# Casting DMAs that wait for transposing DMAs in a two-layer decoder trunk on eight cores

## What is computed

```
for l in (0, 1):
    x = LN(alpha*x + 0.5 * swiglu(x, w_gate_up[l,0], w_down[l,0]))     # hidden width 2816
    y = hgrn2(x) if l == 0 else fox(x, k, v, c)
    x = LN(alpha*x + y)
    x = LN(alpha*x + 0.5 * swiglu(x, w_gate_up[l,1], w_down[l,1]))
    if l == 0: k, v, c = shared_kv(x)
```

## Time and profile before

| | |
|---|---|
| median of 6 runs | 5612.0 us (5487.88 to 5886.92) |
| profiled execution | 5522.29 us |
| its span on the slowest core, core 3 | 5521.2 us |
| TensorE busy | 5221.5 us, 95% of the span |
| VectorE, ScalarE, GpSimd busy | 3078.2, 2092.0, 324.1 us |
| DMA | 958.78 MB, mean 174 GB/s |

### The profile page before, as it was taken

How to read it: one execution, slowest core, us unless ns; L and a number is a source line. 1 busy time by engine, 2 the same in 40 slices (tenths; PEclk the granted TensorE clock), 3 DMA queues, 4 the chain that set the end, 5 groups by cost and what they waited for, 6 DMA issues and landing times.

```text
span 5521.2 us, 74413 instructions; the slowest of 8 cores (5430.5 to 5521.2 us)
## 1 busy us (share of the span) xinstructions
PE 5221.5 (95%) x29504; PEld 2491.6 (45%) x29504; DVE 3078.2 (56%) x5549; ACT 2092.0 (38%) x4106; POOL 324.1 (6%) x500
## 2 busy tenths in 40 slices
PE   5999999889999999699999999999699999999997
PEld 2444444334444444344444445454354544555443
DVE  2466777657867737468453634634435455262565
ACT  0135354435454425344211123254264614746110
POOL 1100000111000001010000000000100000000000
PEclk8999999999999999899999999999899999999999
DMA  9785856995746579876774665947978546373441
GB/s 211 162 204 150 234 152 166 162 239 136 236 109 194 168 203 212 148 196 169 223 198 134 165 179 170 248 125 184 196 188 199 167 146 195 103 222 106 124 153 67
DMA packets 605692, 958.78 MB, mean 174 GB/s; under 512 B 336608, under 2 KB 367008, under 8 KB 594080
## 3 DMA queue, kind: packets, MB, share of 16 engines
q1 hardware_dynamic: 525712, 733.75, 48.9%
q0 software_dynamic: 33552, 94.42, 11.0%
q10 hardware_dynamic: 46080, 125.85, 6.3%
HBM read 722.67 MB, written 266.86 MB: 179 GB/s over the span
## 4 chain that ended last, share of the span: by engine, by line
PE 82%; DMA 7%; ACT 4%; SPq 3%; DVE 2%; issue 1%; POOL 0%; ACTq 0%; DVEq 0%; POOLq 0%
PE pb L621 73%; PE pb L1130 4%; SPq L241 3%; PE pb L1152 2%; DMA xT_6<-o_d 1%; DMA lw_43<-hqf_s 1%; ACT L876 1%; DMA xT_5<-xb_d 1%; DMA o_d<-oall 1%; DMA wgu_s<-wg_7 1%; ACT L713 1%; ACT hlf_2_47 L876 1%; PE pb L1133 1%; DMA wg_7<-w_gu 0%; PE pb L949 0%
## 5 line engine op out<-in xcount | busy, mean ns | idle before, releaser
L621 PE MATMUL pb<-wd,hT_12 128*128 128x512 bf16 x2816 | 652.9, 382 | 24.9 <-DVE rD_17 L745 14.2
L621 PE MATMUL pb<-wd,hT_13 128*128 128x512 bf16 x2816 | 645.5, 379 | 0.2
L713 ACT ACTIVATE sg_14<-pb 128x512 f32<-128x512 f32 x352 | 210.1, 597 | 883.4 <-PE pb L621 881.9
L715 DVE SCALAR_TENSOR_TENSOR sg_14<-sg_14,pb 128x512 f32<-128x512 f32 x352 | 241.5, 686 | 468.9 <-ACT sg_14 L713 468.4
L715 DVE SCALAR_TENSOR_TENSOR sg_15<-sg_15,pb 128x512 f32<-128x512 f32 x352 | 241.5, 686 | 441.8 <-ACT sg_15 L713 441.4
L621 PEld LDWEIGHTS pb<-wd,hT_12 128*128 128x128 bf16 x2816 | 273.0, 98 | 348.8 <-issue 19.5
L713 ACT ACTIVATE sg_15<-pb 128x512 f32<-128x512 f32 x352 | 210.1, 597 | 580.0 <-PE pb L621 577.7
L621 PEld LDWEIGHTS pb<-wd,hT_13 128*128 128x128 bf16 x2816 | 270.5, 98 | 315.1 <-DVE rD_21 L749 1.2
L621 PE MATMUL pb<-xT_3,wg_7 128*128 128x512 bf16 x1408 | 334.2, 384 | 50.1 <-DMA wg_7<-w_gu 48.8
L621 PE MATMUL pb<-xT_3,wg_8 128*128 128x512 bf16 x1408 | 330.5, 381 | 8.7 <-DMA wg_8<-w_gu 6.8
L621 PE MATMUL pb<-xT_4,wg_7 128*128 128x512 bf16 x1408 | 329.0, 380 | 9.6 <-DMA xT_4<-x_t 5.7
(11 more groups left out here) (494 smaller groups left out, 8837.1 us busy)
## 6 DMA issues: line engine op xcount, KB each, us to landing
wd<-wdn_s SPq DMA_DIRECT2D x48, 1024.0 KB, 7.1
wg_9<-wgu_s SPq DMA_DIRECT2D x66, 512.0 KB, 4.4
wg_10<-wgu_s SPq DMA_DIRECT2D x66, 512.0 KB, 4.6
wg_7<-wgu_s SPq DMA_DIRECT2D x66, 512.0 KB, 4.4
wg_8<-wgu_s SPq DMA_DIRECT2D x66, 512.0 KB, 4.7
wd<-w_dn POOLq DMA_DIRECT2D x88, 256.0 KB, 8.4
wd<-wdn_s SPq DMA_DIRECT2D x24, 768.0 KB, 8.0
wdn_s<-wd SPq DMA_DIRECT2D x16, 1024.0 KB, 14.6
```

What stands on the lines that cost most here:

```text
L621: ins = e.matmul(out, lhsT=pairs[i][0], rhs=pairs[i][1], start=(start and i == 0), stop=(stop and i == n - 1))
L713: R.op("act", lambda e, sg=sg, pg=pg: e.activation(out=sg.t[:], in_=pg.t[:], func=AF.Tanh, scale=0.5), reads=[pg.b], writes=[sg.b], cost=c ...
L715: R.op("dve", lambda e, sg=sg, pg=pg: e.scalar_tensor_tensor(out=sg.t[:], in0=sg.t[:], scalar=1.0, in1=pg.t[:], op0=ALU.add, op1=ALU.mult) ...
```

## The change

When the planner takes a casting DMA from POOL's ready list, it looks at the transposing DMAs that it has already placed. If one of them is not over in planned time, the casting DMA is put back until the last of them is over, and other work of POOL may go ahead meanwhile. When it is placed at last, all transposing DMAs that ended in planned time less than 15 us ago become its predecessors, so that on the chip POOL waits for their semaphores. Transposing DMAs that are placed after a casting DMA do not wait for it.

```diff
+XPBACK = 15.0
...
+    xps = []
...
         _, i = heapq.heappop(a)
         o = ops[i]
+        if e == "pool" and o.dma is not None:
+            xps = [x for x in xps if x.end > t - XPBACK]
+            hold = max((x.end for x in xps), default=0.0)
+            if hold > t:
+                o.ready = hold
+                push(o)
+                continue
+            o.preds.update(x.i for x in xps)
+        elif o.xp:
+            xps.append(o)
         o.start = t
```

## The result

The change makes the kernel faster by 0.9%: the changed kernel takes 0.9909 of the time of the kernel before, with a 95% interval of 0.9878 to 0.9941. A later comparison on another chip gave 0.9904 [0.9872, 0.9935]. Its medians, 5657.46 against 5533.48 us, also hold executions lengthened by a lower granted clock, which the ratio leaves out; the others took 5443 to 5486 us, against 5488 to 5544 before. The profiled execution took 5471.22 us against 5522.29, **51 us less**. The forecast was 81 less. Taken of 5522 us, the interval is 33 to 67 us: it holds the 34 us of rival 1, and not the 81.

The account below looks back on a forecast made before the run. TensorE holds 82% of the chain, so time is won only where it stands still. Gains 25 + 31 + 10 + 27 = 93, less 12, give 81 us: 5522 to 5441, plus 90 for the median, 5530; range 5402 to 5625.

Parts of the forecast that it names:

- rival 1: Mere sharing: casts and transposes only divide the DMA engines; half the sum, less 12, 34 us won, 5578 us; chance 0.14.
- A: Place at 1100 us, TensorE stops of 7.90, 14.17 and 4.68 us; forecast gain 25 us, including 2.5 from the clock.
- D: Place at 3960 us, TensorE stop of 34.72 us; SP's transposes to take 7.9 us instead of 35.42, gain 27 us.
- B: Place at 2300 us, TensorE stop of 41.02 us, to become 10 with SP free earlier; gain 31 us.
- C: Place at 3890 us, TensorE stops of 4.68 and 3.81 us; at most 14.8 us to gain, 10 taken.
- a clean place: Window with no cast near, where four transposes were issued and had landed in 7.90 us; forecast for SP at A and D.
- 12 charged for a meeting: Cost of held casts still under way when the next transposes start: one cast out of D's three, 12 us.
- rival 3: Slower: held casts meet the next transposes at B and D, up to 34.72 us each; 66 us slower, 5678 us; chance 0.12.
- the even cores are no floor: Claim that even cores (core 0 5438.2 us, core 3 5521.2) don't limit the gain, having stops of the same kind to lose.
- the cover of 20.7 us: Time until TensorE reaches a wg tile, from four buffers; to cover 8 us of waiting and a clean landing of 6.0.
- the 79 GB/s: DMA rate with transposes and casts both under way, against 163 or 219 for either alone; read as mixing costing capacity.
- Rival 2: The wait misses: casts on the wrong side in planned time aren't held, order only shuffled; 5612 us, give or take 30; chance 0.15.

Follow-up runs that it names:

- e4: Kernel before, planned order unchanged; transposes wait for casts planned before them and not over 15 us ago, casts wait for no transposes; ratio to before 0.9964.
- e1: Kernel before, planned order unchanged, with only the waits of casts for transposes added; ratio to before 0.9891.
- e6: Changed kernel, and transposes also wait for casts that ended in planned time under 15 us before; no ratio, two comparable executions 5478.2 and 5492.1 us.
- e2: Changed kernel without its waits: casts are put back in the plan but wait for no transposes on the chip; ratio to before 0.9925.
- m1: DMA-only kernel, no layer computed: 16 transposes and 12 casting loads; transposes alone 28.8 us, casts alone 42.6, together 68.8 and 61.2.
- m3: DMA-only kernel, four transposes and three casts, with or without eight plain loads; without them 20.4 us for casts during transposes, 20.2 for casts waiting.
- e5: Kernel before, planned order unchanged, with waits in both directions between casts and transposes; ratio to before 0.9951.
- e3: Changed kernel made two-sided: transposes are also put back in the plan and wait for casts; ratio to before 0.9869, again on another chip 0.9887.

## Why the prediction was right, and where its size was off

**Direction and place: right.** TensorE's stops at A to D fell from 111.0 to 34.7 us on the profiled cores; in the mean over all eight, with every pause counted from a place's first transposes of xb_d to 35 us after its last transpose of o_d has landed, they fell from 82.9 to 30.5 us. Of the casts that went out upon running transposes, 30 on each core, 2 or 3 are left. In A, B and C it went as forecast, if not down to the 7.9 us of a clean place. The reverse wait (e4), the only version that neither holds casts back nor lets them wait, keeps 23 of the 30, the stops (89 us) and little gain.

**D: the time came, the way was another.** The forecast kept casts away from D's transposes, with SP at 7.9 us. On every core two to five casts were under way when these started, and SP took 18.2 to 28.7 us (25.9 to 36.2 before). TensorE's long stop went all the same, because it still had work: it was busy for 17.3 to 23.5 us while those transposes were under way, and for 3.7 to 8.3 before, when core 3 had stood from 3950.0 us on and the first of them was issued at 3950.74. Whether TensorE owes that work to the earlier end of C or to the moved order isn't separated. e1 and e6 do in D what the forecast describes (12.3 and 8.5 us of SP), and neither is shown to be faster. So that D's term came near was in part luck.

**The terms.** Worked out as the prediction did, with the slowest core of each profile: A 26.8 - 6.2 = 20.6 (forecast 25), B 41.0 - 8.7 = 32.3 (31), C 8.5 - 5.0 = 3.5 (10), D 34.7 - 14.8 = 19.9 (27). The sum is 76.3, against the 81 forecast with 12 charged for a meeting. Nearly all of the difference is the clock, for which the forecast had some 4 us (2.5 in A, and in C 10 against stops of 8.5). TensorE was busy at half clock for 87.7 us on core 3 before and for 87.6 on core 2 after (72 and 70 in the mean over the cores). In A nothing came back, in C most did, to hold against the earlier trace rows:

```profile
1100.90:1107.70 6.80, 5.89 (x14) 2.05 (x15) 2.28 (x3) 0.00 (x0) 0.00 (x0) 0.50 1.06 310
3845.20:3848.60 3.40, 3.25 (x8) 1.16 (x9) 0.47 (x1) 2.52 (x4) 0.00 (x0) 0.50 0.78 189
```

and stops elsewhere brought half clock of their own (5.77 busy us from 1158.9 to 1172.6). The meeting came, at D, through the mechanism of rival 3: casts not over when o_d's transposes started, four of the five from the burst that C had held. Its price was 10.3 us of TensorE, near the 12 charged and far below that rival's 34.72.

**The term that was left out** stands at "it adds no instruction": the prediction charged nothing for what the change does outside A to D. Stops of 5 us or more there were 8.7, 5.1 and 6.7 us before (at 2185, 3520 and 3837 us on core 3), 20.5 in all; after, on core 2, they are 8.9, 10.3, 6.7, 7.2, 7.4 and 6.6 (at 606, 1156, 2601, 3109, 3487 and 4144), 47.1. That is 26.6 more, and 76.3 - 26.6 = 49.7, against 51 measured. That this comes so near is in part chance, since it sets one core against another and leaves out short pauses: in all, TensorE's idle time fell by 55.0 us and its busy time rose by 4.0. In the mean over the eight cores, every pause counted, A to D gave 52.4 us, the first 580 us gave 5.2, and elsewhere, up to 5300 us, 8.9 were lost (83.6 before, 92.5 after). By e2 and e1 the stops at 606 and 2601 come from the moved order; the others can't be put down to one part. Nothing in the rows of before showed how little slack the loads of lw and rD had. The waits alone have such a cost too: e1 waits 27.9 us for sg and 28.8 for lw in the mean, 15.1 and 16.8 before.

**Which core.** The forecast was made from core 3, which lost most: 116.0 us in A to D by that count, against 82.9 in the mean. In that execution A's collision was on the odd cores alone (25.3 to 41.6 us of SP for four transposes, with four casts upon them; 8.9 to 10.5 on the even ones, with two). Core 3 won 107 us, more than forecast. But the time is the slowest core's. In both profiles one core of each pair (0 and 1, 2 and 3, ...) is some 30 to 90 us slower than the other, not always the same one. The slower ones' mean over the four pairs went from 5510.6 to 5459.3 us, by 51, and that of the faster ones from 5442.8 to 5399.6, by 43. Which core of a pair is the slower one changes between executions of one kernel: before, cores 0 and 1 took 5543.7 and 5481.5 us in one and 5468.2 and 5538.6 in another. So neither core 3's 107 us nor core 2's rise from 5430.5 to 5470.2 is the change's doing alone, and no single core can tell whether "the even cores are no floor" was right.

**The absolute time and the 1%.** The 5530 added 90 us, because the median of the six executions shown stood that far above the profiled one; over twenty executions of the kernel before it stands 11 above. So only the 81 can be held against a measured difference. "Less than that a measurement of this kernel can't tell from none", said of 1%, was wrong: 0.9% is clear of none here. By the prediction's own bound the result is "same", to which it gave 0.22.

**The held casts cost little at POOL**, as forecast: DVE's wait for the power is 22.6 us in 33 waits, 42.3 in 32 before. POOL's waits for transposes were not all under 15 us, though:

```profile
POOL wg_7 L253 <- DMA xT_5<-xb_d: 77.7, 1, 77.7
...
POOL wg_10 L253 <- DMA xT_6<-o_d: 47.0, 2, 23.8
POOL wg_8 L253 <- DMA xT_6<-o_d: 38.4, 1, 38.4
```

(These are POOL's idle times; what ended last is named.) After the wait of 77.7 us the tile landed 86 us before TensorE read it. After the one of 38.4, in D, it landed at 3928.39 us and TensorE read it at 3928.55: the cover of 20.7 us was used up, and no stop came of it by 0.2 us. The one stop for wg in mid-span, 10.3 us, was for a cast that had gone out before the transposes.

**The other signs.** TensorE's wait for xT_6 is under 30 us, as forecast (28.9). SP is under 12 us at one of the four places with four transposes (10.34; 12.55, 13.04 and 28.72). The casts of wd in C land in 17.1 us, not in under 15: they meet one another and the next transposes. And one sign of being wrong came, TensorE's wait for wg in mid-span: on one core in the first profile, on two and four in the later ones, 5.0 to 11.6 us each.

**Mixing costs capacity: half right.** The prediction took the 79 GB/s as what mixing costs, and so set rival 1, mere sharing, aside. By themselves the kinds share: 68.8 and 61.2 us against a sum of 71.4 in m1, 20.4 against 20.2 us in m3 whether the casts wait or not. What the wait does there is to give the transposes the engines first, 9.1 us instead of 20.4, and the casts have slack. The Trainium skill, "DMA: Bandwidth & Descriptors", section "Issuing engines are not separate DMA queues", has DMAs of all issuing engines interleave on the same engines, and these runs agree with it. By the time alone rival 1 is as near as the forecast: it has 34 us, the measured is 51. But it let half of the stops remain, and 34.7 of 111.0 did. In the kernel crawling stretches fell too, from a mean of 62 us to 31, and before they were 90 and 82 us on cores 3 and 1, the slowest two, and 38 and 40 on cores 0 and 4. So both are seen at work. How much of the gain each has isn't settled: e5 and e3 have the same crawl, 30, at 0.9951 and 0.9869, and e1 wins as much as the changed kernel with a crawl of 44. Why a stretch crawls on one core and not on another stays open as well.

**Rival 2, the miss,** did not come about: 2 or 3 of the 30 casts upon transposes are left. In the old order the waits alone do miss 17 of them (e1), and still have the whole gain; those that they hit lie in A, B and D, in D two of three on every core.

## What to carry to other kernels

Don't price a change by the stops of the core that happens to be the slowest: compare all cores, and expect from the change what the mean of the slow ones wins. When two kinds of DMA collide, let the one that TensorE is about to need go first, and look for the cheapest form of it: here added waits alone, or a moved order alone, did about what both did together. Ask too whether TensorE has other work while a transfer is slow: in D the transposes stayed slow and the stop went, and e6 made them fast and won nothing more. A moved order or an added wait can make TensorE wait somewhere else, so charge for that; here 9 us of a 52 us gain were lost so in the mean over the cores, and 27 of 76 by the slowest.

## What the runs showed of the hardware

- Transposing DMAs came last beside weight loads that were issued with them: 16 of them took 28.8 us alone and 68.8 and 61.2 beside 12 casts that took 42.6 alone and 47.0 and 42.3 beside them. Beside 12 loads that cast nothing, 24.0 us alone, they took 47.8, and the loads 29.0. Plain loads of the same rows were through before the casts, after 37.2 us of 52.7.
- Who comes second matters: casts upon running transposes took 23.5 and 26.7 us, transposes upon running casts 18.8, the sum of both alone is 21.6. On another chip the first took 20.4, and by core it took from 16.2 to 30.5 us in all.
- The DMA engines can be counted as fully busy and yet nearly stand still. Here is B on the slowest core, in 40 slices of 1 us (busy tenths, then GB/s). Before, from 2257 to 2297 us:

```profile
DMA  9999994999999999999999999991999999999999
GB/s 207 205 303 418 410 200 35 50 70 65 76 131 120 131 133 110 140 163 84 94 68 61 62 65 71 70 139 37 60 48 51 52 49 53 54 32 57 29 64 65
```

and after, from 2241 to 2281 us:

```profile
DMA  9999999899959499999797998979998999999999
GB/s 166 182 283 416 426 237 110 98 77 116 120 105 252 85 98 300 403 276 211 74 90 61 115 147 104 141 104 190 180 117 223 299 290 237 250 236 244 210 229 213
```

Before, 20 of the last 22 slices stay below 85 GB/s, and the busy tenths are at 9 in all of those but one; after, the last ten slices are at 210 to 299.
